# A two-block network on one core: the panels of weights taken out of DeltaNet's inversion levels, five gate panels at DeltaNet's end

## The reference

```python
(z_s, xbc, dt_s, qkv, z_d, b_d, a_d, gate_s, gate_d) = jnp.split(u @ w_in[l], split_points, axis=-1)
y_s = mamba2_branch(z_s, xbc, dt_s, ...)
y_d = deltanet_branch(qkv, z_d, b_d, a_d, ...)
merged = (jax.nn.sigmoid(gate_s) * (y_s @ ssm_w_branch[l])
          + jax.nn.sigmoid(gate_d) * (y_d @ dn_w_branch[l]))
```

```python
M = jnp.where(strict, jnp.einsum("bnhid,bnhjd->bnhij", kb, k) * decay, 0.0)
sol = lax.linalg.triangular_solve(eye + M, rhs, left_side=True, lower=True, unit_diagonal=True)
```

## Time and profile before

| | us |
|---|---|
| median of 3 runs (2267.79 to 2276.11) | 2271.68 |
| the profiled execution, its own time | 2272.29 |
| its span | 2270.5 |
| mean granted clock of PE | 0.977 of full |
| busy: PE, DVE, ACT | 2151.0, 1330.3, 1138.3 |

### The profile page before, as it was taken

How to read it: one execution, slowest core, us unless ns; L and a number is a source line. 1 busy time by engine, 2 the same in 40 slices (tenths; PEclk the granted TensorE clock), 3 DMA queues, 4 the chain that set the end, 5 groups by cost and what they waited for, 6 DMA issues and landing times. The chain is left out here.

```text
span 2270.5 us, 40909 instructions
## 1 busy us (share of the span) xinstructions
PE 2151.0 (95%) x15620; PEld 1881.5 (83%) x15620; DVE 1330.3 (59%) x1845; ACT 1138.3 (50%) x1681; POOL 61.5 (3%) x74
## 2 busy tenths in 40 slices
PE   6999889999999999988999999999999997999998
PEld 4787778887888987988998887888997796998887
DVE  3446365556556976574655555555896576556555
ACT  3454544445445556653545445444556663535444
POOL 0000000000000010000000000000002000000000
PEclk8999999999999999998999999999999998999999
DMA  9662245545554544321455554554454421254553
GB/s 399 242 240 97 88 143 188 188 179 185 185 185 145 180 145 148 146 76 57 149 186 193 185 185 171 187 193 166 155 185 131 149 100 70 90 186 180 189 190 121
DMA packets 53328, 373.24 MB, mean 164 GB/s; under 512 B 6304, under 2 KB 6304, under 8 KB 9280
## 3 DMA queue, kind: packets, MB, share of 16 engines
q1 hardware_dynamic: 47664, 342.00, 41.7%
q0 software_dynamic: 5520, 29.23, 3.6%
HBM read 370.10 MB, written 1.11 MB: 163 GB/s over the span
## 5 line engine op out<-in xcount | busy, mean ns | idle before, releaser
L1418 ACT ACTIVATE HI<-ring 128x1024 fp32r<-128x1024 f32 x606 | 625.1, 1054 | 765.7 <-PE banks L537 399.2
L1962 DVE TENSOR_TENSOR LO<-ring,HI 128x1024 fp32r<-128x1024 f32 x318 | 389.1, 1226 | 369.6 <-ACT HI L1418 369.3
L1968 DVE TENSOR_TENSOR LO<-ring,HI 128x2048 fp32r<-128x2048 f32 x139 | 318.5, 2292 | 250.8 <-ACT HI L1418 245.3
L501 PE MATMUL banks<-UH,HI 128*128 128x256 f32 x1392 | 409.4, 294 | 0.0
L502 PE MATMUL banks<-UL,HI 128*128 128x256 f32 x1392 | 398.3, 286 | 0.0
L503 PE MATMUL banks<-UH,LO 128*128 128x256 f32 x1392 | 397.7, 286 | 0.0
L535 PE MATMUL banks<-HI,UH 128*128 128x512 f32 x896 | 350.0, 391 | 7.1 <-DVE LO L1968 5.0
L536 PE MATMUL banks<-LO,UH 128*128 128x512 f32 x896 | 349.4, 390 | 0.0
L537 PE MATMUL banks<-HI,UL 128*128 128x512 f32 x896 | 349.3, 390 | 0.0
L501 PEld LDWEIGHTS banks<-UH,HI 128*128 128x128 f32 x1392 | 271.5, 195 | 18.8 <-issue 17.7
L502 PEld LDWEIGHTS banks<-UL,HI 128*128 128x128 f32 x1392 | 271.9, 195 | 1.4 <-issue 1.2
(11 more groups left out here) (325 smaller groups left out, 3094.6 us busy)
## 6 DMA issues: line engine op xcount, KB each, us to landing
ring<-in_w_stream SPq DMA_DIRECT2D x315, 1024.0 KB, 4.8
ARENA<-in_ada_stream POOLq DMA_DIRECT2D x16, 1024.0 KB, 5.2
ARENA<-in_ada_stream SPq DMA_DIRECT2D x8, 1024.0 KB, 14.9
GRMS<-cum_rows POOLq DMA_DIRECT2D x16, 256.0 KB, 3.6
ARENA<-in_na_bias POOLq DMA_DIRECT2D x2, 1024.0 KB, 13.6
RMS<-cum_rows POOLq DMA_DIRECT2D x8, 256.0 KB, 3.4
RSTD<-cum_rows POOLq DMA_DIRECT2D x8, 256.0 KB, 3.7
ARENA<-in_ropes POOLq DMA_DIRECT2D x1, 1088.0 KB, 19.1
```

Of the source, the lines that this page charges most:

```text
L501: nc.tensor.matmul(out, lh, rh, start=start, stop=False, **kw)
L1418: nc.scalar.activation(HI[:, q % PARTS, at], ring[:, q % RING, at], ACT.Copy).then_inc(hi_ready, 1)
L1962: nc.vector.tensor_tensor(LO[:, q % PARTS, at], ring[:, q % RING, at], HI[:, q % PARTS, at].bitcast(F32), ALU.subtract).then_inc(lo_ready, 1)
L1968: nc.vector.tensor_tensor(LO[:, q % PARTS, :], ring[:, q % RING, :], HI[:, q % PARTS, :].bitcast(F32), ALU.subtract).then_inc(lo_ready, 2)
```

## The change

- `head_sums2(0)` moves from turn j = 1 to j = 2 of the z_s loop, behind that turn's panel.
- No panel is left inside the levels. Late panel 4 comes at their end: its first half before the last `inverse_turn`, its second half after `last_u(1)`. The four halves among the steps of the state are now those of panels 5 and 6, and five panels (7 to 11, `END_GATES = 5`) instead of four stand at DeltaNet's end.
- At the end, the sum of squares and the two spreads stand between the halves of panels 7, 8 and 9 instead of behind panels 8, 9 and 10.
- The four `group_norm` leave the levels on DVE: two go in after `new_values`, two after the last `late_low` of the state's steps. `late_gate` and `late_low` leave the levels too.
- ACT takes the root of the sums after YSH 1 instead of after YSH 3, and DVE the reciprocal after YSL 1 instead of after YSL 7; the remaining `late_gate` and `late_low` are spread among the steps of YD.
- The copy of the transpose in the last level becomes three operations instead of four.

```diff
-LEVEL_PANELS = {3: (L_ZD, 0), 7: (L_ZD, 1), 11: (L_ZD + 1, 0), 15: (L_ZD + 1, 1)}
-END_GATES = 4
+END_GATES = 5
...
-                    if 1 <= j <= 4:
-                        mm = head_sums2(j - 1)
+                    if 2 <= j <= 4:
+                        for c in (0, 1) if j == 2 else (j - 1,):
+                            mm = head_sums2(c)
                         if j % 2 == 0:
...
                     if n:
                         inverse_turn(n - 1)
-                    if n in LEVEL_PANELS:
-                        late_wide(*LEVEL_PANELS[n])
+                late_wide(L_ZD, 0)
                 inverse_turn(UNITS_DN - 1)
                 last_u(0)
                 last_u(1)
+                late_wide(L_ZD, 1)
                 for g in range(4):
                     last_v(g)
                     if g + 2 < 4:
                         last_u(g + 2)
                 new_values(0)
                 new_values(1)
-                late_wide(L_ZD + 2, 0)
+                late_wide(L_ZD + 1, 0)
                 chunk_state(0)
                 chunk_state(1)
                 outputs(0)
                 outputs(1)
-                late_wide(L_ZD + 2, 1)
+                late_wide(L_ZD + 1, 1)
                 keys_state(0)
                 keys_state(1)
-                late_wide(L_ZD + 3, 0)
+                late_wide(L_ZD + 2, 0)
                 new_values(2)
                 new_values(3)
-                late_wide(L_ZD + 3, 1)
+                late_wide(L_ZD + 2, 1)
                 outputs(2)
                 outputs(3)
 
                 for j in range(END_GATES):
-                    late_panel(L_ZD + L_GATES - END_GATES + j)
+                    late_wide(L_ZD + L_GATES - END_GATES + j, 0)
                     if j == 0:
                         pe.wait_ge(osq_ready, 4 * l + 4)
                         for h in range(DN_HEADS):
...
                         else:
                             pe.wait_ge(yd_ready, 4 * l + 2)
                         spread_rows(j - 1, OROOT, O_BANKS).then_inc(ob_done, 1)
+                    late_wide(L_ZD + L_GATES - END_GATES + j, 1)
...
-                        for r in range(2):
-                            for b in range(2):
-                                w = r ^ b
-                                ins = nc.scalar.activation(tiles(TT[part64(b), g, :], 4)[:, 2 * w:2 * w + 2, part64(b)],
-                                                           tiles(bank_pair[3][part64(b), r, 0:P], 2), ACT.Copy)
+                        first = tiles(TT[part64(0), g, :], 4)[:, :, part64(0)].rearrange("p (w j) n -> p w j n", w=2)
+                        nc.scalar.activation(first, bank_pair[3][part64(0), :, 0:P].rearrange("p w (j n) -> p w j n", j=2), ACT.Copy)
+                        for w in range(2):
+                            ins = nc.scalar.activation(tiles(TT[part64(1), g, :], 4)[:, 2 * w:2 * w + 2, part64(1)],
+                                                       tiles(bank_pair[3][part64(1), 1 - w, 0:P], 2), ACT.Copy)
                     ins.then_inc(turn_ready, 1)
...
-                    if n == 8:
-                        late_gate(L_ZD)
-                    if n == 16:
-                        late_gate(L_ZD + 1)
                     inverse_turned(n)
...
+                late_gate(L_ZD)
                 state_in(0)
                 state_in(1)
                 output_in(0)
                 output_in(1)
+                late_gate(L_ZD + 1)
                 late_gate(L_ZD + 2)
-                late_gate(L_ZD + 3)
                 output_in(2)
                 output_in(3)
                 act.wait_ge(o_copied, 4 * l + 4)
...
                                          ACT.Copy).then_inc(branch_hi, 1)
                     if j == 3:
                         late_gate(L_ZD + L_GATES - END_GATES)
+                    if j == 1:
                         act.wait_ge(oss_done, l + 1)
                         nc.scalar.activation(OROOT, bank[6][:, 0:S], ACT.Sqrt, bias=EPST[:, :], scale=1.0 / P).then_inc(orms_ready, 1)
-                for j in range(1, END_GATES - 1):
-                    late_gate(L_ZD + L_GATES - END_GATES + j)
                 for j in range(4):
+                    if j % 2 == 0:
+                        late_gate(L_ZD + L_GATES - END_GATES + 1 + j // 2)
                     act.wait_ge(yd_ready, 4 * l + j + 1)
                     nc.scalar.activation(YDH[:, 2 * j:2 * j + 2, :], QKV[:, 2 * j:2 * j + 2, :],
                                          ACT.Copy).then_inc(branch_hi, 1)
+                late_gate(L_ZD + L_GATES - 2)
...
                     if n + 2 < UNITS_DN:
                         inverse_masked(n + 2)
-                    if n in (10, 18):
-                        late_low(L_ZD + (n - 10) // 8)
-                    if n % 4 == 3 and n < 4 * GROUPS:
-                        group_norm(n // 4)
                 new_values(0)
                 new_values(1)
+                group_norm(0)
+                late_low(L_ZD)
+                group_norm(1)
                 dve.wait_ge(v_taken, 4 * l + 4)
                 right_side(0)
                 right_side(1)
-                late_low(L_ZD + 2)
+                late_low(L_ZD + 1)
                 new_values(2)
                 new_values(3)
-                late_low(L_ZD + 3)
+                late_low(L_ZD + 2)
+                group_norm(2)
+                group_norm(3)
 
                 def branch_low(i, low, high, x_):
                     dve.wait_ge(branch_hi, 12 * l + i + 1)
...
                 for j in range(8):
                     at = slice(2 * j, 2 * j + 2)
                     branch_low(j, YSL[:, at, :], YSH[:, at, :], CONV[:, at, :])
+                    if j == 1:
+                        dve.wait_ge(orms_ready, l + 1)
+                        nc.vector.reciprocal(OROOT, OROOT).then_inc(or_ready, 1)
                     if j == 3:
                         late_low(L_ZD + L_GATES - END_GATES)
-                dve.wait_ge(orms_ready, l + 1)
-                nc.vector.reciprocal(OROOT, OROOT).then_inc(or_ready, 1)
-                late_low(L_ZD + L_GATES - END_GATES + 1)
                 for j in range(4):
                     dve.wait_ge(ob_done, 2 * l + j // 2 + 1)
                     x_ = QKV[:, 2 * j:2 * j + 2, :]
...
                                                              bank[O_BANKS[j % 2 * 2 + e]][:, 0:S], ALU.mult, ALU.mult)
                     need(step(ins))
                     nc.vector.tensor_tensor(x_, x_, ZD[:, 2 * j:2 * j + 2, :], ALU.mult).then_inc(yd_ready, 1)
-                late_low(L_ZD + L_GATES - END_GATES + 2)
+                    if j == 1:
+                        late_low(L_ZD + L_GATES - END_GATES + 1)
                 for j in range(4):
                     at = slice(2 * j, 2 * j + 2)
                     branch_low(8 + j, YDL[:, at, :], YDH[:, at, :], QKV[:, at, :])
+                    if j % 2:
+                        late_low(L_ZD + L_GATES - END_GATES + 2 + j // 2)
```

## The result

| | before | after |
|---|---|---|
| median of 6 runs each, us | 2272.55 | 2257.99 |
| ratio, 95% interval | | 0.993 (0.9915 to 0.9946) |
| span of the profiled execution, us | 2270.5 | 2254.4 |
| granted clock of PE | 0.977 | 0.984 |

The kernel is faster by 14.6 us; forecast were 17 (2255 us). The total came out near the forecast in part by luck: several terms erred in opposite directions. Code lines up to L1155 are one lower than before, and the panel's matmuls are L500 to L502.

What follows compares the result with a forecast made beforehand. PE, busy for 95% of the span, was taken to bound the kernel. The terms -2.4 - 25.5 - 3.0 + 14.4 = -16.5 us took 2272.3 to 2255.8, stated as 2255 us, range 2247 to 2268.

Steps and rivals of the forecast that it cites:

- levels: First v to `new_values`: 39.6 and 38.8 us against 52.07 and 51.78, together -25.5 us.
- first `new_values`: Behind the levels: full clock expected after a half panel, -1.3 and -1.7, together -3.0 us.
- from there to X: Up to the last half panel's end among the state's steps: the added DVE and ACT work is covered, no change.
- X to the last gate panel: From the last half panel's end among the state's steps: 40.3 us against 33.13, +14.4 us for both layers.
- more than three gaps a layer: Sign of being wrong: PE idle inside a block with nothing releasing it, above three times a layer; two were taken.
- The first rival: Levels: short supply of PE's own list, 8 gaps a layer instead of 2, +14.3 us, 2269 us; chance 0.05.
- second rival: Levels: PE at half clock throughout, units 1.33 instead of 1.20 us, +5.7 us a layer, 2266 to 2267; chance 0.07.
- third rival: Levels: units behind missing half panels cost their hidden wait again, 4 x 1.2 a layer, +9.6 us, 2265; chance 0.06.
- Norms: Levels: the four `group_norm` on DVE would cost 3.4 us each if left in without the half panels.
- Last level: End of the levels: three ACT copies about 0.9 us against 1.12; turn to turn 1.8 at half clock against 2.03.
- The fourth rival: DeltaNet's end: DVE's row later than 23.4 us; the gain is gone at 8.3 us a layer more; chance 0.04.
- First z_s panel: Behind the last plain panel: PE waits 2.56 us for LO instead of 3.75 for ACT's squares, -2.4 us together.

Runs made afterwards that it cites:

- norms_in: The changed kernel with the four `group_norm` back in DVE's row of the levels, no panels there: 2273.38 us, ratio 1.0006 to the kernel before.
- copies_4: The changed kernel with the last level's copy of the transpose as four operations again instead of three: 2259.77 us, ratio 0.9944 to the kernel before.
- halves_mid: The changed kernel with late panel 4's two halves behind units 5 and 11 of the levels instead of at their end: 2264.75 us.
- the repeat: The changed kernel with empty instructions added in the levels that never reached the chip, so an exact repeat: 2259.01 us, ratio 0.9938 to the kernel before.
- sums_back: The changed kernel with `head_sums2(0)` back in turn j = 1 of the z_s loop: 2264.35 us, ratio 0.9966 to the kernel before.
- transposes: The changed kernel with four of the eight products of each `inverse_turn` as transposes: 2332.61 us, ratio 1.0263 to the kernel before.

## Why the prediction came out

| term, both layers | forecast | profile |
|---|---|---|
| last plain panel to first v | -2.4 | -3.7 |
| levels | -25.5 | -19.5 |
| first `new_values` | -3.0 | -2.8 |
| from there to X | 0 | -1.0 |
| X to the last gate panel | +14.4 | +10.2 |
| sum | -16.5 | -16.7 (span -16.1) |

The terms missed by -1.3, +6.0, +0.2, -1.0 and -4.2, which nearly cancel: that the total came out within 3 us is luck. Of the levels' 19.5 us, 12.2 are four half panels in both layers that went elsewhere, and the end pays for them with 12.0; what the reordering itself gains is 7.3 in the levels and 1.8 at the end, besides the other terms. By the prediction's own signs the levels were wrong: more than three gaps a layer was one of being wrong, and 38 to 41 us from the first v to `new_values` one of being right, where it was 43.0 and 41.4.

**Levels: direction right, size wrong.** The failed step is "The first layer shows one in five stretches without a panel, the second two. I take two in each, 2.4 us." I counted gaps in the levels of before, where a half panel, a norm or a gate every fourth unit gave the supply time; these were the cover, not the stretches between. Measured: 5.7 us a layer instead of 2.4. That is as much as the 3.3 us between 39.2 forecast and 42.5 measured, on the mean of both layers; the smaller misses in the levels cancel. The first rival had the mechanism and overshot with 8 gaps, 2269; its line for four gaps a layer, 2260, is near what was measured. Slow clock was below the 1.5 us taken: 10.3 us at half clock in one layer, about 1.0 us of loss by 1.33 against 1.20 a unit, and none in the other.

**Half clock through the levels** (second rival): did not happen for long. Twenty units ran at 1.00 in the second layer; in the first the clock fell to 0.50 twice, for 6.9 and 3.4 us, each time after the longest gaps (1.51 and 1.58 us), and came back. Of the twelve stretches nine have 3 to 14 us at half clock, and none is slow throughout. The rival's "waiting fills a third of a unit" was too much: the profile counts PE busy in 1.02 of the 1.20 us. The Trainium skill's rule (TensorE: Matmul & The Clock Gate, "A second HAM failure mode: psum-queue depth-cycling") has such an engine swing between the two levels. The traces agree that it swings, but show far less of it than the rival's price took; in the second layer of the changed kernel they show none. **Panels as cover** (third rival): the v to v of 1.20 us stayed without them; as cover against short supply they did matter, which I had not joined up. **Norms**: "with the halves gone and the norms left in, they would cost 3.4 each": up to 3.6 by norms_in.

**Last level.** Three copies were forecast to lower turn to turn to 1.8; the rows show 1.76 and 1.68 on ACT (L1818 at 1025.83, 1027.59, 1029.27). The cause was only partly the copies: with four of them, copies_4 has 2.03 and 1.79. That the rest of the better end of the levels is the half panel that stands in for a wait, and the clock, is what halves_mid shows.

**First `new_values`**: right, 1.81 for 1.7; halves_mid shows that the half panels ahead are the reason.

**DeltaNet's end.** The row of DVE was worked out rightly: reciprocal done at 14.0 us from X (forecast 14.4), two quarters at 22.8 (23.4). The waits are 0.60 and 2.12 (1.0 and 2.3). The term "with a slow stretch behind the second wait as now (1.2)" did not come true in this execution; the repeat has it in one layer, sums_back in both (1.5 us each). Of the 16 such stretches with a wait of 2.1 us there, in eight programs, 8 have it. It is an even chance and not a fixed cost, and before it was paid in both layers. The fourth rival (the row late by 8 us) had no support.

**First z_s panel.** Wait 2.62 for 2.56 forecast. "The slow clock behind the wait I leave as it is" failed: it is gone in 20 of the 24 stretches above, and in one layer of the profiled execution.

What stays open: why a gap ends 1.2 to 1.5 us after its piece has landed, and why the same gap differs (0.5 to 1.6 us), or is missing, between executions of one program.

## What to carry to other kernels

Count instructions as well as time. PE starved here where it ran through 256 entries in 3.0 us (64 x 64 fp32 products) and got the next 256 some 4.2 us after the last; a panel, 96 entries in 6.0 us, leaves no such gap. There an instruction costs more than its time on the engine: 16 entries more a unit, 0.14 us of PE, cost 0.30. Long matmuls in between earn back a part (two half panels 3.1 of 5.7 us a layer, one 0.8). A stretch measured between fillers doesn't tell what it costs without them: gap counts must be taken per entry issued, not per unit shown. Before work is moved off a path, look for idle time of the engine that it goes to at exactly the row where it lands; one norm moved into 4.3 us of idle time was worth 2.2 us a layer, 4 us of the kernel.

## What the runs showed of the hardware

- Short matmuls were bound by the delivery of PE's instructions: 256 entries, 16 KB, came every 3.7 to 4.8 us (4.2 on the mean), one transfer at a time of 0.9 to 1.4 us. At 102 entries in 1.20 us this costs 13% of the levels.
- (Run transposes.) A transpose and a plain fp32 product in turn cost 0.64 us a pair, at half clock, against 0.11 for two plain products at half clock and 0.07 at full; whether the transpose or the alternation costs it, and why the clock stayed at 0.50, wasn't tried.
- Dense panels between short, waiting blocks kept the granted clock at 1.00 through `last_v` and `new_values`; without them it was 0.66 and 0.50 from the last v on, and 0.50 in `new_values`, in both layers.
